# A state-space scan whose decay weights move from VectorE to ScalarE, one way at a time, with buffers three deep

## What is computed

```python
a = (dt * A);  a_cum = jnp.cumsum(a, axis=-1)
lmat = jnp.exp(segsum(a))
cb = jnp.einsum('bclgn,bcsgn->bgcls', cc, bc)
y_diag = jnp.einsum('bgcls,bgrcls,bcsgrp->bclgrp', cb, lmat, xc)   # xc = x * dt
...
y_off = jnp.einsum('bclgn,bcgrpn,bgrcl->bclgrp', cc, prev_states, jnp.exp(a_cum))
...
y = y_f + flip(y_b) + d_skip.astype(f32).reshape(g, r)[:, :, None] * xs
gated = y.reshape(bsz, length, g, r * p) * jax.nn.silu(zs.astype(f32)).reshape(bsz, length, g, r * p)
gated = gated * lax.rsqrt(jnp.mean(gated * gated, axis=-1, keepdims=True) + EPS)
```

## Time and profile before

| what | us |
|---|---|
| median of 3 runs | 3101.01 (3096.8 to 3103.73) |
| the profiled execution's own time | 3098.0 |
| its span in the trace | 3095.9 |
| the scan, from its first load to its last store issued | 804.0 to 1109.2 |
| of it, from the first to the last product with M starting | 836.7 to 1095.7 |

### The profile page before, as it was taken

The page is one execution under the profiler, slowest core; times in us unless marked ns, Lnnn a source line. Parts: engine busy times, 40 slices in busy tenths (PEclk is TensorE's granted clock), DMA queues, the critical chain, the costliest instruction groups (busy, mean ns, idle before and its releaser), DMA issues.

```text
span 3095.9 us, 35168 instructions
## 1 busy us (share of the span) xinstructions
PE 2754.6 (89%) x12924; PEld 2207.4 (71%) x12924; DVE 2152.0 (70%) x2892; ACT 1280.4 (41%) x2069; POOL 774.9 (25%) x385
## 2 busy tenths in 40 slices
PE   6999989979588869969979996989899489999998
PEld 3788767755365658858767875777788478888887
DVE  5589865526689944854634898973555479999997
ACT  3233321110166631223224214666532067777775
POOL 1432310000111100000210006555200035566664
PEclk9999999988798889989989998999999689999999
DMA  6222347633454452326543247441232289999996
GB/s 224 77 70 84 104 148 239 204 126 124 158 184 169 176 229 68 102 56 153 105 116 83 99 112 135 110 121 25 89 123 97 116 310 381 381 383 384 388 381 222
DMA packets 236294, 530.82 MB, mean 171 GB/s; under 512 B 30742, under 2 KB 147590, under 8 KB 219859
## 3 DMA queue, kind: packets, MB, share of 16 engines
q1 hardware_dynamic: 173058, 435.96, 40.2%
q0 software_dynamic: 33680, 58.97, 7.8%
q10 hardware_dynamic: 29376, 33.56, 3.1%
HBM read 450.74 MB, written 95.48 MB: 176 GB/s over the span
## 4 chain that ended last, share of the span: by engine, by line
PE 51%; DVE 6%; POOL 2%; ACT 2%; DMA 2%; issue 1%; SPq 1%; DVEq 0%; ACTq 0%; POOLq 0%
PE banks L143 47%; PE banks L153 4%; DVE a_P L2163 1%; DVE c_rows L1518 1%; POOL a_P L2187 1%; ACT a_PT L2206 1%; DVE m_w_low L1621 0%; DVE e_low L2666 0%; POOL a_R L1551 0%; DMA i_q<-iqT 0%; DVE a_R L1556 0%; ACT m_w_low L1614 0%; DMA p_low_raw<-in_w_out 0%; DMA odsaT<-a_o 0%; ACT e_high L2660 0%
## 5 line engine op out<-in xcount | busy, mean ns | idle before, releaser
L2666 DVE TENSOR_TENSOR e_low<-e_raw,e_high 128x4096 fp32r<-128x4096 f32 x99 | 437.9, 4425 | 64.1 <-ACT e_high L2660 64.1
L143 PE MATMUL banks<-m_w_low,p_high 128*128 128x512 f32 (+1 forms) x1248 | 381.0, 389 | 13.3 <-DVE m_w_low L1621 13.3
L2660 ACT ACTIVATE e_high<-e_raw 128x4096 fp32r<-128x4096 f32 x99 | 359.5, 3633 | 26.9 <-DVE e_g L2615 26.9
L143 PE MATMUL banks<-h_high,w 128*128 128x512 f32 (+1 forms) x1024 | 297.9, 373 | 9.1 <-POOL w L373 4.4
L505 DVE SCALAR_TENSOR_TENSOR acc<-img,taps,acc 128x1024 f32<-128x1024 f32 x160 | 259.8, 1625 | 61.6 <-ACT acc L483 56.6
L143 PEld LDWEIGHTS banks<-m_w_low,p_high 128*128 128x128 f32 x1248 | 234.3, 195 | 57.4 <-issue 8.7
L143 PE MATMUL banks<-m_w_low,p_low 128*128 128x512 f32 (+1 forms) x624 | 240.5, 385 | 0.0
L143 PEld LDWEIGHTS banks<-h_high,w 128*128 128x128 f32 x1024 | 186.2, 191 | 49.0 <-POOL w L373 4.9
L143 PE MATMUL banks<-e_high,e_xhigh 128*128 128x512 f32 x528 | 211.5, 401 | 7.1 <-issue 5.5
L143 PE MATMUL banks<-e_high,e_xlow 128*128 128x512 f32 x528 | 208.3, 395 | 0.0
L143 PE MATMUL banks<-e_low,e_xhigh 128*128 128x512 f32 x528 | 207.9, 394 | 0.0
(11 more groups left out here) (495 smaller groups left out, 6245.5 us busy)
## 6 DMA issues: line engine op xcount, KB each, us to landing
e_raw<-in_exp_w SPq DMA_DIRECT2D x99, 2048.0 KB, 13.0
s_sums<-cumT SPq DMA_DIRECT2D x32, 768.0 KB, 4.5
w_raw<-in_w_in SPq DMA_DIRECT2D x20, 1024.0 KB, 6.2
s_X<-xtok SPq DMA_DIRECT2D x19, 1024.0 KB, 7.3
p_raw<-in_w_in SPq DMA_DIRECT2D x18, 1024.0 KB, 7.3
w_raw<-in_ada_w SPq DMA_DIRECT2D x12, 1024.0 KB, 5.4
mod_w<-in_ada_w SPq DMA_DIRECT2D x12, 1024.0 KB, 6.9
w_raw<-in_w_ada SPq DMA_DIRECT2D x10, 1024.0 KB, 8.1
```

The costliest lines, as they stand in the source:

```text
L143: last = pe.matmul(out, a, b, start=start and n == 0, stop=stop and n == len(pairs) - 1)
L2660: act.activation(self.high[p % HIGHS][:], self.raw[p % RAWS][:], ACT.Copy).then_inc(*self.high_done.up())
L2666: dve.tensor_tensor(self.low[p % HIGHS][:], self.raw[p % RAWS][:], self.high[p % HIGHS][:].bitcast(F32), ALU.subtract).then_inc(*self.low_ ...
```

## The change

The decay weights are built for each way by itself. For each way and head ScalarE takes Relu(off - sum), where off is the running sum plus 60 minus the logarithm of dt (new table, made in Transforms), in place in the buffer of sums; then one exponential of 60 minus that, over all 12 x 128 columns, writes M. VectorE multiplies M in place with the masked pairs. dt is thus inside M, X is used as it is, and `timed` and its two buffers go. The scaling of the state parts moves from ScalarE (12 instructions) to VectorE (2). The sums and M have three buffers, the scaled parts two. Sums are loaded five steps ahead in place of two, each once the exponential of three steps before has freed its buffer. The product with H for step n + 1 is issued in step n, and every engine's order in the loop changes as shown. GpSimd's product with the decays is left out for the last chunk. `roots` is renamed `squares`, `part(n)` is a slice of group n's 384 columns, `flat(tile)` a view without inner dimensions.

```diff
+TINY, CEILING = 1e-37, 60.0
...
@@ steps_and_sums @@
+        dve.tensor_scalar(self.t["off"][:], self.t["dt"][:, 0:NT, :], TINY, None, ALU.max).then_inc(*vec.up())
+        act.wait_ge(*vec.at(6))
+        act.activation(self.t["off"][:], self.t["off"][:], ACT.Ln).then_inc(*self.logged.up())
...
@@ decays @@
-        dve.tensor_tensor(t["gap"][:], p[:, 0:NT, 0:NH], p[:, 0:NT, NH:2 * NH], ALU.subtract).then_inc(*vec.up())
-        dve.tensor_scalar(t["back"][:], p[:, 0:NT, NH:2 * NH], -1.0, None, ALU.mult).then_inc(*self.tables_done.up())
+        dve.wait_ge(*self.logged.at(1))
+        dve.scalar_tensor_tensor(out=t["off"][:], in0=p[:, 0:NT, :], scalar=CEILING, in1=t["off"][:], op0=ALU.add, op1=ALU.subtract).then_inc(*vec.up())
+        dve.memset(t["ceiling"][:], CEILING).then_inc(*self.tables_done.up())
...
@@ state_space @@
-        t.update({k: s.sb("s_" + k, [P, NT, NH]) for k in ("gap", "back")})
+        t["off"], t["ceiling"] = s.sb("s_off", [P, NT, 2 * NH]), s.sb("s_ceiling", [P, 1])
...
-        sums = [s.sb(f"s_sums{b}", [P, 2, HG, P]) for b in range(2)]
-        xfs = [[s.sb(f"s_xf{b}{w}", [P, DS]) for w in range(2)] for b in range(2)]
-        E = [s.sb(f"s_E{b}", [P, HG, P]) for b in range(2)]
-        M = [[s.sb(f"s_M{b}{w}", [P, HG, P]) for w in range(2)] for b in range(2)]
+        sums = [s.sb(f"s_sums{b}", [P, 2, HG, P]) for b in range(3)]
+        M = [s.sb(f"s_M{b}", [P, 2, HG, P]) for b in range(3)]
-        y2 = [s.sb(f"s_y2{w}", [P, 384]) for w in range(2)]
+        y2 = [[s.sb(f"s_y2{b}{w}", [P, 384]) for w in range(2)] for b in range(2)]
...
         def load_sums(n):
 
             c, g = n // NBC, n % NBC
-            if n >= 2:
-                sp.wait_ge(*diffed.at(n - 1))
-            sp.dma_start(sums[n % 2][:].rearrange("p w h n -> p w (h n)"),
-                         row(dram["cumT"][c, :, HG * P * g:HG * P * g + HG * P])).then_inc(*sums_in[n % 2].up())
+            if n >= 3:
+                sp.wait_ge(*exped.at(n - 2))
+            sp.dma_start(sums[n % 3][:].rearrange("p w h n -> p w (h n)"),
+                         row(dram["cumT"][c, :, HG * P * g:HG * P * g + HG * P])).then_inc(*sums_in[n % 3].up())
 
...
-                sp.wait_ge(*timed_done.at(2 * c - 2))
...
-        def differences(n):
+        def depths(n):
 
             c, g = n // NBC, n % NBC
-            dve.wait_ge(*sums_in[n % 2].at(n // 2 + 1))
-            if n >= 2:
-                dve.wait_ge(*M_done.at(n - 1))
-            for h in range(HG):
-                last = dve.scalar_tensor_tensor(out=E[n % 2][:, h, :], in0=sums[n % 2][:, 0, h, :], scalar=col("gap", c, HG * g + h),
-                                                in1=sums[n % 2][:, 1, h, :], op0=ALU.subtract, op1=ALU.min)
-            last.then_inc(*diffed.up())
+            act.wait_ge(*sums_in[n % 3].at(n // 3 + 1))
+            for w in range(2):
+                for h in range(HG):
+                    last = act.activation(sums[n % 3][:, w, h, :], sums[n % 3][:, w, h, :], ACT.Relu, bias=col("off", c, NH * w + HG * g + h), scale=-1.0)
+            last.then_inc(*bounded.up())
 
         def exponents(n):
+
+            act.wait_ge(*bounded.at(n + 1))
+            if n >= 3:
+                act.wait_ge(*summed.at(n - 2))
+            act.activation(flat(M[n % 3]), flat(sums[n % 3]), ACT.Exp, bias=t["ceiling"][:, 0:1], scale=-1.0).then_inc(*exped.up())
+
+        def weights(n):
+
             c, g = n // NBC, n % NBC
-            act.wait_ge(*diffed.at(n + 1))
-            for h in range(HG):
-                last = act.activation(E[n % 2][:, h, :], E[n % 2][:, h, :], ACT.Exp, bias=col("back", c, HG * g + h))
-            last.then_inc(*E_done.up())
-
-        def weights(n):
-            c, g = n // NBC, n % NBC
-            dve.wait_ge(*E_done.at(n + 1))
+            dve.wait_ge(*exped.at(n + 1))
             dve.wait_ge(*cb_done.at(c + 1))
-            if n >= 2:
-                dve.wait_ge(*summed.at(n - 1))
             for w in range(2):
-                last = dve.tensor_tensor(M[n % 2][w][:], E[n % 2][:], over(cbs[c % 2][:, w, g, :], 1, HG), ALU.mult)
+                last = dve.tensor_tensor(M[n % 3][:, w, :, :], M[n % 3][:, w, :, :], over(cbs[c % 2][:, w, g, :], 1, HG), ALU.mult)
             last.then_inc(*M_done.up())
-
-        def timed(w, c):
-            b = c % 2
-            dve.wait_ge(*X_in[b].at(c // 2 + 1))
-            if c >= 2:
-                dve.wait_ge(*summed.at(4 * c - 4))
-            dve.tensor_tensor(heads(xfs[b][w][:]), heads(Xs[b][:, 0:DS]), over(col("dt", c, NH * w, NH), 2, HP), ALU.mult).then_inc(*timed_done.up())
 
...
         def scale(n):
 
             c, g, y0 = n // NBC, n % NBC, 2 + 3 * (n % 2)
-            act.wait_ge(*off_summed.at(n + 1))
-            if n:
-                act.wait_ge(*summed.at(n))
+            dve.wait_ge(*off_summed.at(n + 1))
+            if n >= 2:
+                dve.wait_ge(*summed.at(n - 1))
             for w in range(2):
-                for h in range(HG):
-                    at = slice(HP * h, HP * h + HP)
-                    last = act.activation(y2[w][:, at], core.bank[:, y0 + 1 + w, at], ACT.Copy, scale=col("ec", c, NH * w + HG * g + h))
+                last = dve.tensor_tensor(heads(y2[n % 2][w][:]), heads(core.bank[:, y0 + 1 + w, 0:384]), over(col("ec", c, NH * w + HG * g, HG), 2, HP), ALU.mult)
             last.then_inc(*scaled.up())
 
         def within_chunk(n):
             c, g, y0 = n // NBC, n % NBC, 2 + 3 * (n % 2)
             pe.wait_ge(*M_done.at(n + 1))
-            pe.wait_ge(*timed_done.at(2 * c + 2))
+            pe.wait_ge(*X_in[c % 2].at(c // 2 + 1))
             if n >= 2:
                 pe.wait_ge(*gathered.at(n - 1))
             for h in range(HG):
                 c0 = HP * (HG * g + h)
                 for w in range(2):
-                    pe.matmul(core.bank[:, y0, HP * h:HP * h + HP], M[n % 2][w][:, h, :], xfs[c % 2][w][:, c0:c0 + HP], start=h == 0 and w == 0, stop=False)
+                    pe.matmul(core.bank[:, y0, HP * h:HP * h + HP], M[n % 3][:, w, h, :], Xs[c % 2][:, c0:c0 + HP], start=h == 0 and w == 0, stop=False)
 
...
@@ skip_and_weigh @@
+            if c < NT - 1:
...
@@ vector_step @@
             dve.wait_ge(*stepping.at(n + 1))
+            dve.wait_ge(*off_summed.at(n + 1))
...
-        load_chunk(0), load_sums(0), load_sums(1)
+        load_sums(0), load_chunk(0), load_sums(1)
         sp.dma_start(skip[:], row(dram["d_skip"])).then_inc(*rows_in.up())
         sp.dma_start(nw[:], row(dram["ssd_norm_w"])).then_inc(*rows_in.up())
-        load_chunk(1), load_z(0)
+        load_sums(2), load_chunk(1), load_z(0), load_sums(3), load_sums(4)
         pool.wait_ge(*rows_in.at(2))
         dve.wait_ge(*rows_in.at(2))
-        tensor_pairs(0), skip_and_weigh(0), skip_and_weigh(1)
-        differences(0), exponents(0), differences(1), exponents(1), timed(0, 0), timed(1, 0), vector_pairs(0), weights(0)
+        tensor_pairs(0), from_states(0), skip_and_weigh(0), skip_and_weigh(1)
+        depths(0), depths(1), exponents(0), depths(2), exponents(1), vector_pairs(0), scale(0), weights(0)
         for n in range(N + 1):
             c, g = n // NBC, n % NBC
+            if n < N:
+                within_chunk(n)
+                if n + 1 < N:
+                    from_states(n + 1)
+                if n < STEPS:
+                    tensor_step(n)
+                both(n)
+            if n + 3 < N:
+                depths(n + 3)
+            if n + 2 < N:
+                exponents(n + 2)
+            if n + 5 < N:
+                load_sums(n + 5)
+            if n + 1 < N:
+                weights(n + 1)
             if n:
                 gather(n - 1)
-                if n - 1 < N - NBC:
+                if n - 1 < STEPS:
                     vector_step(n - 1)
-            if n < N:
-                from_states(n), scale(n), within_chunk(n)
-                if n < N - NBC:
-                    tensor_step(n)
-                both(n)
             if n + 1 < N:
-                weights(n + 1)
-            if n + 2 < N:
-                load_sums(n + 2), differences(n + 2), exponents(n + 2)
+                scale(n + 1)
             if g == 0 and c:
-                gate(c - 1), roots(c - 1)
+                gate(c - 1), squares(c - 1)
             if g == 1 and c:
                 if c + 1 < NT:
                     load_chunk(c + 1)
...
                 norm(c - 1), store(c - 1)
                 if c + 1 < NT:
                     skip_and_weigh(c + 1)
-            if g >= 2 and c + 1 < NT:
-                timed(g - 2, c + 1)
             if g == 2 and c + 1 < NT:
                 vector_pairs(c + 1)
         norm(NT - 1), store(NT - 1)
```

(4 more changed lines are left out.)

27 lines of the change are left out of this document (15 added, 12 removed).

## The result

The changed kernel took 3156.13 us (median of 4 runs, 3155.7 to 3158.58) where the kernel before took 3099.95 (4 runs, 3096.8 to 3103.73): 1.018 times as long, 95% interval 1.0168 to 1.0193. It is slower, by 56 us where 35 were forecast, and 3 us above the range. The profiled execution took 3156.36 (span 3154.3), so the two profiled executions stand 58 us apart.

What follows compares the result with a forecast made beforehand. VectorE was taken as the fullest engine, TensorE close behind. From 3098.0 us, -10.8 (start) + 51.8 (six chunks) - 5.9 (end) gave 3133.1, and 3 more for the median 3136; range 3101 to 3153.

Steps and rivals of the forecast that it cites:

- What bounds the kernel before: Scan: VectorE is fullest, busy 29.5 of 33 us, TensorE next with 28.6; chunks 1 to 6 take 34.56 us each.
- The new wait: TensorE idles 12 us ahead of tensor_pairs: SyncE asks for B and C at 17.85, behind load_sums; they land at 23.85.
- The half clock after it: TensorE after the load wait runs at half clock: pairs 1.85 us, product with M to 30.85, from_states to 33.3.
- Gathers and steps the state (41.2): VectorE, late in the chunk: after M of step n + 4 (39.7), gather and state step end at 41.2 us.
- tensor_step 0.7 and `both` 1.3 end at 43.2: TensorE's last work of a chunk: next chunk starts at 43.2 us in place of 34.56, six times, +51.8.
- if TensorE waits elsewhere: Sign that the forecast is wrong: TensorE waits somewhere other than ahead of tensor_pairs for the load into s_xb.
- The start: First product with M at 825.9 against 836.66, minima and weighting of X gone: -10.8 us (-5.8 to -15.8).
- The end: Steps 28 to 31, without the load of a next chunk: 15.6 us against 21.5, -5.9.
- The rest at nothing: Logarithm in the stage before costs 0 to 1 us; tail after the scan the same, loads and bytes as before.
- (a): Rival: the wait is there but the clock recovers at once; 38.7 us a chunk, about 3109 in all; chance 0.15.
- (b): Rival: SyncE's load is not late and only ScalarE's block stays; 30.7 us a chunk, 3061 in all; chance 0.12.
- (c): Rival: Relu needs another table set than the exponential, two loads of 1.3 a step on ScalarE; 3147; chance 0.05.

Runs made afterwards that it cites:

- b1: Kernel before with only the scaling of the state parts moved from ScalarE (twelve instructions) to VectorE (two): 3101.01 us, beside 3102.45 unchanged.
- e1: Changed kernel with the load of the next chunk's B, C and X asked for ahead of the load of sums: 3066.28 us.
- e4: Changed kernel with ScalarE's squares of the finished chunk one step later, behind the exponential that SyncE waits for: 3075.38 us.
- e3: Changed kernel with 13 added products of 128x512, results dropped, keeping TensorE busy while it would wait for B and C: 3135.72 us.
- e2: Changed kernel with three buffers of y in place of two, so GpSimd's skip product does not wait for the store: 3137.82 us.
- e6: e5 with GpSimd's product of X and the skip weights replaced by a fill with zero: 3047.3 us.
- c_after: Changed kernel run again unchanged, as a control: 3158.67 us, beside 3098.01 for the kernel before.
- e5: Changed kernel with the chunk's load ahead of the sums, squares and store each one step later, three buffers of y: 3048.95 us, 0.9833 of the kernel before.

## Why the prediction was too small, point by point

**What bounds the kernel before:** right in the main. b1, where VectorE got more and ScalarE less, did not get faster, and VectorE stood at 95%; but of 3.2 us more a chunk only 0.6 showed.

**The new wait:** right in place, cause and size. B and C were asked for 17.88 after the chunk's first product (forecast 17.85) and landed after 6.0 (5.8 to 6.3 in the six chunks); pairs came at 24.05 (23.85). Relus 3.60 and the exponential of 1536 columns 1.57, as estimated. e1 and e4 each take the wait away from another end, and 90 and 81 us of the time with it.

**The half clock after it:** right. Pairs 2.04 and product 5.22 (1.85 and 5.15 forecast), granted 0.50 until close to 888, 10 us after the work resumed. Its worth was put at 4.5 us a chunk (43.2 less 38.7). e3 gained 3.2, and 4.4 in chunk 2 if the half clock that came at that chunk's end is taken off (43.8 less 39.4, an estimate from e3). The one exception is chunk 4 (41.1), where the clock came back earlier and the product took 3.67.

**"Gathers and steps the state (41.2)" and "tensor_step 0.7 and `both` 1.3 end at 43.2":** these are the terms that failed. Up to M the sum holds well: from_states ends at 33.8 (33.3), norm at 37.1 (36.7), masked pairs at 38.35 (37.9), M at 40.2 (39.7). From there two costs were missing: in chunk 1 the state step ends at 44.3 in place of 41.2, and the next chunk starts at 48.1 in place of 43.2. The first cost is GpSimd: its skip product is freed by the chunk's store, comes just as VectorE makes the decay, and the decay takes 3.00 in place of 0.55, 2.4 more. The second follows from the first: half clock comes again after TensorE's idle of 4.42, and tensor_step with `both` takes 3.70 to the next product (898.06 to 901.76) where full clock needs 2.0. That is 1.7; together 43.8 becomes 48, in four chunks of six. The collision stood in the bounds of the range with 2.8 and on another instruction (M), and the second half clock nowhere; e2 removes both, and the mean chunk goes from 46.19 to 43.98. So of the 18 us missing in the chunks 13.3 are these two costs, and 4.7 are the 0.8 a chunk by which the rest of the chain was sized too small. The recorded sign "if TensorE waits elsewhere" came true here: it waited 4.2 to 4.7 us ahead of tensor_step in the four long chunks. A bound should have been followed on to what it sets off.

The Trainium skill (SBUF — State Buffer, Who interferes with whom) says that a VectorE instruction with two SBUF inputs contends with a GpSimd instruction that reads SBUF, not with one that only writes it. The decay of 3.00 beside GpSimd's product and the 4.06 of e6 in place of 6.70, where the product is a fill, agree.

**The start:** -10.8 forecast, -11.9 measured at the first product and -13.1 at step 4, well inside -5.8 to -15.8. **The end:** -5.9 forecast, -5.1 measured in the profiled execution, -1.3 in c_after (20.18 against 21.48), so it is not firm. **The rest at nothing:** the span behind step 31 grew by 6.9, where two executions of one kernel differ by up to 2.9 (2000.2 and 2003.1 before); the cause stays open. This term was put at 0 to 1.

**The sum:** forecast -10.8 + 51.8 - 5.9 = +35.1; measured -13.1 + 69.8 - 5.1 + 6.9 = +58.5 in the profiled executions. Of the 23.4 missing, 18.0 lie in the chunks, 6.9 behind the scan and 0.8 in the last steps, less 2.3 that the start gained more. The 3 us added for the median were not there after: the profiled execution (3156.36) and the median (3156.13) agree.

**The rivals.** (a), full clock at once, did not happen: each of the six waits for s_xb (11.4 to 11.9) was followed by pairs of 2.04 to 2.05 in place of 1.05. (b) did not happen, since the queue's order stood against it as the forecast said, and its price was about right: e1 gave 31.74 against 30.7 a chunk, 3066 against 3061. (c): no table load is recorded on the Relus' line; the loads on the lines of the exponential and of the root are as many as before.

## What to carry to other kernels

Where a queue issues its loads in order, a load takes on every wait of the loads ahead of it: ask for the next tile's inputs ahead of any load that waits for a buffer, and compare the time of issue with the consumer's. If work moves from the full engine to an emptier one, follow the order on the new engine's queue too, since the sums by engine (26 to 27 here) are a floor, which e5 came near (29) once fewer queues waited for another's late item. Chunks of two lengths in one loop are a reason to look for two engines that meet at nearly the same time; here a further buffer took that meeting off the path.
